# Where the small level products of a GLA head are issued: in one block, or in pieces between the steps of a tile

## The chip, the cores and the metric

The kernel runs on one core of a Trainium2 chip. The metric is the device time of one execution in microseconds (us), as the median of several runs. TensorE (PE in the profile) does matrix products, and its weight loads have an engine name of their own there (PEld). VectorE is DVE, ScalarE is ACT, GpSimd is POOL, and SyncE (SP) issues most of the weight transfers.

## The reference

One inference step of a two-layer decoder trunk, for 512 prompt tokens and 32 sample tokens (8 sequences of 4) with shared weights, in float32. Each layer is a SwiGLU block, a mixing block of three branches (mLSTM, gated linear attention, RG-LRU), an output projection, and a second SwiGLU block. The change touches gated linear attention (GLA), which has four heads with key width 128 and value width 256:

```python
def _gla(q, k, v, log_a, S0):
    ...
    def step(S, inp):
        qc, kc, vc, ac = inp
        b = jnp.cumsum(ac, axis=2)
        diff = jnp.where(causal[:, :, None], b[:, :, :, None, :] - b[:, :, None, :, :], -jnp.inf)
        A = jnp.einsum('bhtd,bhsd,bhtsd->bhts', qc, kc, jnp.exp(diff))
        o = jnp.einsum('bhts,bhsv->bhtv', A, vc) + jnp.einsum('bhtd,bhdv->bhtv', qc * jnp.exp(b), S)
        bL = b[:, :, -1]
        S_new = jnp.exp(bL)[..., None] * S + jnp.einsum('bhsd,bhsv->bhdv', kc * jnp.exp(bL[:, :, None] - b), vc)
        return S_new, o
```

The scores A have a decay for each key dimension, so they aren't one plain product of q and k.

## The kernel before, in words

All 544 tokens are kept with features on the partitions. A large weight product is made of three passes over split operands (high and low parts, `xh`, `xl`, `wh`, `wl`). Its unit is a tile: 128 output features for all 544 tokens, in 8 steps over the inner dimension, each step six matmuls of 272 columns (three passes, two halves), all at L415. `pair` holds two PSUM buffers for tiles, `stream_a` and `stream_b` in the profile, and `Q` (`mix` in the profile) is the PSUM of the attention work, four banks.

Every engine has its own order of instructions, written out by hand, and the engines meet through semaphores that count up. A weight block of 1 MB holds two tiles. SyncE loads it into `stage` when VectorE has split the block before last in that slot; ScalarE copies the high part (`split_hi`, L836), VectorE makes the low part (`split_lo`, L1154), and TensorE multiplies.

A GLA head takes four weight blocks: n (query and key tiles), n + 1 (values), n + 2 and n + 3 (four gate tiles, t + 4 to t + 7). The attention work lies between these tiles. The scores are made by levels. A chunk of 128 tokens is halved again and again, and at each level a product of decayed queries and decayed keys (`seven`, one row for each level) gives the scores across the cut. The two coarsest levels are the outer products (L690). The diagonal (`kT` and `qT`) and the five finest levels are six inner products (L698); each is 16 small matmuls of 32 by 32 outputs, 4 chunks by 4 groups of `G` = 32 rows, and each matmul shows as two records. Behind them come the sample sequences' products (L702 to L706) and a transpose of the decayed keys into rows (L710). All of this is one function, `scores`, that is called between tile t + 4 and tile t + 5. Then TensorE issues tile t + 5, waits for `b_took`, and multiplies the key rows with the values (L716) for the states; then tile t + 6 follows, and in `outputs` the next head's decays (L663), the chunk outputs (L723, L725) and the reads of the sample states (L543), which wait for `b_zin`.

VectorE waits for the pieces by `b_ring`, through `ring(0)` to `ring(3)`: it copies the outer products into `wS` (L1571), collects the inner levels with predicated copies into `inner` (L1573, L1578), copies them to `wS` (L1581), copies the key rows to `Kw` (L1583), and handles the samples (L1586 to L1590). The last of these raises `b_took`. Then it merges the previous head (L1396, L1397), takes the gate tile (L1145), updates the states (L1362, L1364), splits a block (L1154), prepares the sample keys, and takes the next head's decays (`take_decays`, L1494), which raises `b_zin`; that step reads the bank that L543 writes next.

`pair_block` already has an argument `inside`: for each of the two tiles a list of a step number and a function to call ahead of that step. The mLSTM heads and tile t + 7 of the GLA heads use it.

Of the kernel before, what the change touches and what calls it, by code (L numbers as in the profile page):

```python
# [27 lines left out]
P = 128  # L28
D = 1024
KT = D // P  # L30
# [10 lines left out]
C = 128  # L41
NC = T // C
# [3 lines left out]
NL = len(LEVELS)  # L46
SM = DV + P
NLS = 2
G = 32
NIN = sum(h < G for h in LEVELS)  # L50
# [33 lines left out]
def spread(ap, dim, n):  # L84

    shape = list(ap.shape)
    shape[dim] = n
    return ap.broadcast_to(shape)


class Chain:
# [22 lines left out]
    def link(self, ins):  # L114
        self.n += 1
        ins.then_inc(self.sem, 1)
        self.eng.wait_ge(self.sem, self.n)
# [5 lines left out]
def trunk(nc, x_T, w_up1, w_down1, w_mix, w_gates, w_o, w_up2, w_down2, vec, b_if, w_lr2, w_ra, w_ri, consts, level_masks,  # L123
          m0, c0, n0, s0, h0, conv0, o_y, o_pc, o_pm, o_ps, o_ph, o_pconv,
          o_sc, o_sn, o_sm, o_ss, o_sh, o_sconv, rows_dram):
    with ExitStack() as ctx:
# [11 lines left out]
        wh = sb("wh", [P, 2, W_SLOT], F32R)  # L138
        wl = sb("wl", [P, 2, W_SLOT], F32R)
        V = sb("vectors", [P, V_ALL])  # L140
        ones = sb("ones", [P, P])
        ident = sb("ident", [P, P])
# [46 lines left out]
        qT = sb("qT", [P, N], where=heads)  # L189
        kT = sb("kT", [P, N], where=heads)  # L190
# [3 lines left out]
        seven = sb("seven", [P, NL, N], where=heads)  # L194
        wS = sb("wS", [P, N], where=heads)
        Kw = sb("Kw", [P, NC, P], where=heads)
# [39 lines left out]
        Q = psum("mix", [P, 4, 512])  # L236
# [49 lines left out]
        b_fac, b_ring, b_took = sem("b_factors"), sem("b_ring_full"), sem("b_ring_took")  # L286
# [123 lines left out]
        def _(pe):  # L410
# [101 lines left out]
            def pair_block(n, t, j, after_first=None, inside=((), ())):  # L512

                block_ready(n)
                for e in range(2):
                    done = 0
                    for k, between in inside[e]:
                        tile(t + e, e, KT, 2 * P, e * P, weights=(wh[:, j], wl[:, j]), ks=range(done, k))
                        between()
                        done = k  # L520
                    tile(t + e, e, KT, 2 * P, e * P, weights=(wh[:, j], wl[:, j]), ks=range(done, KT))
                    if after_first and e == 0:
                        after_first()
# [143 lines left out]
            def gla_head(L, i, first=False, last=False):  # L667
                B = L * HEADS + i
                n = L * LAYER_BLOCKS + i * HEAD_BLOCKS + (BLK_MIX + HEADS * HEAD_BLOCKS)
                t = L * LAYER_TILES + i * HEAD_TILES + (TILE_MIX + GATE_TILES + HEADS * HEAD_TILES)  # L670

                if first:
                    pe.wait_ge(root_done, L * (2 * HEADS) + HEADS + 1 + i)
                    decays(B, 0)
                pair_block(n, t, 0)
                block_ready(n + 1)
                value_tiles(t + 2, 1)
                sm = slice(T, N)

                def scores():  # L680


                    pe.wait_ge(b_fac, B + 1)
                    pe.wait_ge(root_done, L * (2 * HEADS) + HEADS + 1 + i)
                    for c in range(NC):
                        for l, groups in ((0, (0, 1)), (1, (0, 2))):
                            for g in groups:
                                k0, q0 = c * C + g * G, c * C + (g // (2 - l) * (2 - l) + 2 - l if l else 2) * G
                                q1 = q0 + LEVELS[l]
                                mm = pe.matmul(Q[g * G:(g + 1) * G, 0, q0:q1], seven[:, l, k0:k0 + G],  # L690
                                               seven[:, l, q0:q1], start=True, stop=True)
                    mm.then_inc(b_ring, 1)
                    for r in range(NIN + 1):
                        lhs, rhs = (kT, qT) if r == 0 else (seven[:, NL - NIN + r - 1, :],) * 2
                        for c in range(NC):
                            for g in range(P // G):
                                k0, o = c * C + g * G, r % 4 * P + c * G
                                mm = pe.matmul(Q[g * G:(g + 1) * G, 1 + r // 4, o:o + G], lhs[:, k0:k0 + G],  # L698
                                               rhs[:, k0:k0 + G], start=True, stop=True)
                        if r == 3:  # L700
                            mm.then_inc(b_ring, 1)
                    pe.transpose(Q[0:NS, 2, 2 * P:3 * P], kh[:, sm], ident[:])  # L702
                    pe.matmul(Q[0:NS, 2, 3 * P:3 * P + NS], kT[:, sm], qT[:, sm], start=True, stop=True)
                    for e in range(NLS):
                        lv = seven[:, NL - NLS + e, sm]
                        mm = pe.matmul(Q[0:NS, 2, 3 * P + (e + 1) * NS:3 * P + (e + 2) * NS], lv, lv, start=True, stop=True)  # L706
                    mm.then_inc(b_ring, 1)
                    for c in range(NC):
                        sl = slice(c * C, (c + 1) * C)
                        mm = pe.transpose(Q[:, 3, sl], kh[:, sl], ident[:])  # L710
                    mm.then_inc(b_ring, 1)

                pair_block(n + 2, t + 4, 0, scores)
                pe.wait_ge(b_took, B + 1)
                for c in range(NC):
                    pe.matmul(Q[:, c, 0:DV], Kw[:, c, :], val[:, c, 0:DV], start=True, stop=True).then_inc(b_u, 1)  # L716

                def chunk_outputs(v):

                    vs = slice(v * P, (v + 1) * P)  # L720
                    for c in range(NC):
                        sl = slice(c * C, (c + 1) * C)
                        mm = pe.matmul(Q[:, v, sl], val[:, c, vs], wS[:, sl], start=True, stop=c == 0)  # L723
                        if c:
                            mm = pe.matmul(Q[:, v, sl], Cst[:, c - 1, vs], qs[:, sl], start=False, stop=True)  # L725
                    return mm

                def outputs():
                    pe.wait_ge(b_c, B * NC + NC)
                    if not last:  # L730
                        decays(B + 1, 2)
                    chunk_outputs(0)
                    pe.wait_ge(b_cs, B * 16 + 16)
                    if not last:
                        pe.wait_ge(b_zin, B + 2)
                    state_reads(3, b_rd)
                    chunk_outputs(1).then_inc(b_out, 1)
                    pe.wait_ge(b_rows_read, B + 1)
                    for v in range(2):
                        pe.matmul(Q[:, 2, v * NS:(v + 1) * NS], val[:, NC, v * P:(v + 1) * P], wSs[:],  # L740
                                  start=True, stop=False, skip_group_check=True)
                        mm = sample_states(2, v, v * NS)
                    mm.then_inc(b_outs, 1)
                    pe.wait_ge(b_keys, B + 1)
                    sample_updates(0, 3, b_us)

                taken = L * (8 * HEADS) + i * 4 + (4 * HEADS + 1)

                def second():
                    pe.wait_ge(b_h, B + 1)  # L750
                    sample_updates(1, 2, b_us)

                def third():
                    pe.wait_ge(b_sqs, B + 1)
                    column_sum(hsq[:, 0], 0, b_var)
                    pe.wait_ge(head_samples, taken + 1)
                    sample_updates(2, 3, b_us)

                pair_block(n + 3, t + 6, 1, outputs, ((), ((4, second), (6, third))))
                pe.wait_ge(head_samples, taken + 2)  # L760
                sample_updates(3, 2, b_us)
# [370 lines left out]
        def _(dve):  # L1132
# [370 lines left out]
            def gla_head(L, i, first=False, last=False):  # L1503
# [49 lines left out]
                def ring(r):  # L1553
                    dve.wait_ge(b_ring, B * 4 + (r + 1))

                def chunks(ap):

                    return ap.rearrange("p (c t) -> p c t", c=NC)

                def compact(r):  # L1560

                    return chunks(Q[:, 1 + r // 4, r % 4 * P:(r % 4 + 1) * P])
# [6 lines left out]
                for rows, cols_ in ((slice(0, 2 * G), slice(2 * G, P)), (slice(0, G), slice(G, 2 * G)),  # L1569
                                    (slice(2 * G, 3 * G), slice(3 * G, P))):  # L1570
                    dve.tensor_copy(av[rows, :, cols_], src[rows, :, cols_])  # L1571
                ring(1)
                link(tt_(inner[:], compact(0), spread(ident_g[:].unsqueeze(1), 1, NC), ALU.mult))  # L1573
                for r in range(1, NIN + 1):
                    if r == 4:
                        ring(2)
                        chain.hold()
                    link(dve.copy_predicated(inner[:], spread(masks[:, r - 1, :].unsqueeze(1), 1, NC), compact(r)))  # L1578
                for g in range(P // G):
                    rows = slice(g * G, (g + 1) * G)  # L1580
                    dve.tensor_copy(av[rows, :, rows], inner[rows])  # L1581
                ring(3)
                dve.tensor_copy(Kw[:], chunks(Q[:, 3, :]))  # L1583
                As = wSs[0:NS]
                s0_ = 3 * P
                link(tt_(As, Q[0:NS, 2, s0_:s0_ + NS], ident[0:NS, 0:NS], ALU.mult))  # L1586
# [320 lines left out]
```

## Time and profile before

| what | value |
|---|---|
| median of 3 runs | 3126.54 us (3124.81 to 3127.68) |
| profiled execution, its own time | 3129.91 us |
| span of that profile | 3128.1 us |
| TensorE busy | 3055.7 us (98%) |
| VectorE busy | 1902.3 us (61%) |
| ScalarE busy | 1038.8 us (33%) |
| mean granted clock of TensorE | 0.994 |
| DMA | 292.18 MB, mean 93 GB/s |

The profile is one execution. "Busy" is the time in which an engine has at least one instruction under way. The start of an instruction is measured; the end of a matmul is modelled, so distances between starts say more than durations. The granted clock is a share of 2.4 GHz. In the chain, a row gives when a piece of the chain begins, how long it is, and how many records it holds; "issue" is time in which the engine waits for nothing that the profile shows. Some matmul records are missing from the trace, so the counts of such pieces can be a little low.

### The profile page before, as it was taken

Reading aid. Unit: us, or ns where it says so; the run is one execution under the profiler, and the core shown is the slowest. Engines: PE = TensorE matmul, PEld = TensorE weight load, DVE = VectorE, ACT = ScalarE, POOL = GpSimd, SP = SyncE. Lnnn points to the kernel's source line nnn. Section 1 sums busy time; section 2 is a strip of 40 time slices with the busy share of each in tenths; the row PEclk is TensorE's granted clock in tenths of the full one; section 3 lists DMA queues with packets and bytes.
Section 4 is the critical chain, followed back from the end, with each engine's and each line's share of the span. In section 5 each row is a group of like instructions: output and inputs, shape, how many; then the busy total and the mean of one; then the engine's idle time right before and its main releaser. Section 6 shows DMA issues by size and latency. Waiting matters only on the chain.

```text
span 3128.1 us, 60370 instructions
## 1 busy us (share of the span) xinstructions
PE 3055.7 (98%) x25824; PEld 3013.2 (96%) x25824; DVE 1902.3 (61%) x2705; ACT 1038.8 (33%) x992; POOL 12.9 (0%) x36
## 2 busy tenths in 40 slices
PE   7999999999999999999999999999999999999998
PEld 7999999999999999999999999999999999999997
DVE  5434467778887874434454344776888788643344
ACT  3222232334344642212232122333334355421212
POOL 1000000000000000000000000000000000000000
PEclk9999999999999999999999999999999999999999
DMA  4222233233222222222222222233222322222222
GB/s 145 74 99 89 72 112 109 106 110 110 96 100 88 74 83 94 78 97 75 87 94 81 101 89 84 94 125 129 94 89 95 96 91 74 96 81 83 92 79 71
DMA packets 51916, 292.18 MB, mean 93 GB/s; under 512 B 9385, under 2 KB 12265, under 8 KB 23881
## 3 DMA queue, kind: packets, MB, share of 16 engines
q1 hardware_dynamic: 37152, 241.43, 22.3%
q10 hardware_dynamic: 13984, 48.48, 4.2%
q8 instruction: 90, 1.47, 0.2%
q0 software_dynamic: 656, 0.52, 0.1%
q14 instruction: 34, 0.27, 0.0%
HBM read 268.90 MB, written 21.50 MB: 93 GB/s over the span
## 4 chain that ended last, share of the span: by engine, by line
PE 84%; DVE 9%; ACT 4%; issue 2%; DMA 1%; ACTq 0%; DVEq 0%; POOL 0%; POOLq 0%
PE stream_b L415 36%; PE stream_a L415 35%; PE stream_a L502 4%; DVE wl L1154 1%; DVE xc L1653 1%; ACT wh L836 1%; PE stream_b L508 1%; PE mix L622 1%; PE mix L562 1%; PE mix L723 1%; PE mix L543 1%; PE mix L625 1%; ACT L1059 0%; PE mix L555 0%; PE mix L698 0%
## 5 line engine op out<-in xcount | busy, mean ns | idle before, releaser
L836 ACT ACTIVATE wh<-stage 128x2048 fp32r<-128x2048 f32 (+2 forms) x246 | 435.8, 1772 | 773.9 <-PE stream_b L415 561.3
L1154 DVE TENSOR_TENSOR wl<-stage,wh 128x2048 fp32r<-128x2048 f32 (+2 forms) x248 | 525.8, 2120 | 112.2 <-ACT wh L836 88.4
L415 PE MATMUL stream_a<-xh,wh 128*128 128x272 f32 x2560 | 537.5, 291 | 27.0 <-DVE xl L1160 13.0
L415 PE MATMUL stream_b<-xh,wh 128*128 128x272 f32 x2560 | 538.3, 291 | 2.1 <-issue 1.2
L415 PE MATMUL stream_a<-xl,wh 128*128 128x272 f32 x2560 | 531.3, 289 | 0.0
L415 PE MATMUL stream_b<-xl,wh 128*128 128x272 f32 x2560 | 531.3, 289 | 0.0
L415 PE MATMUL stream_a<-xh,wl 128*128 128x272 f32 x2560 | 529.8, 288 | 0.0
L415 PE MATMUL stream_b<-xh,wl 128*128 128x272 f32 x2560 | 529.7, 288 | 0.0
L415 PEld LDWEIGHTS stream_a<-xh,wh 128*128 128x128 f32 x2560 | 404.6, 189 | 31.3 <-DVE wl L1154 13.0
L415 PEld LDWEIGHTS stream_b<-xh,wh 128*128 128x128 f32 x2560 | 405.4, 189 | 8.4 <-issue 3.7
L415 PEld LDWEIGHTS stream_b<-xh,wl 128*128 128x128 f32 x2560 | 404.1, 189 | 1.0 <-issue 1.0
L415 PEld LDWEIGHTS stream_a<-xh,wl 128*128 128x128 f32 x2560 | 404.1, 189 | 0.0
L415 PEld LDWEIGHTS stream_a<-xl,wh 128*128 128x128 f32 x2560 | 401.5, 190 | 0.0
L415 PEld LDWEIGHTS stream_b<-xl,wh 128*128 128x128 f32 x2560 | 401.5, 190 | 0.0
L1145 DVE TENSOR_TENSOR us<-stream_b,rstd 128x544 f32<-128x544 f32 x88 | 63.8, 725 | 446.6 <-PE stream_b L415 446.5
L893 ACT ACTIVATE sg<-gs 128x544 f32<-128x544 f32 x88 | 58.1, 660 | 400.6 <-DVE gs L1145 400.6
L415 PE MATMUL stream_a<-hh,wh 128*128 128x272 f32 x704 | 145.9, 289 | 0.0
L415 PE MATMUL stream_b<-hh,wh 128*128 128x272 f32 x704 | 145.9, 289 | 0.0
L415 PE MATMUL stream_a<-hh,wl 128*128 128x272 f32 x704 | 145.7, 288 | 0.0
L415 PE MATMUL stream_b<-hh,wl 128*128 128x272 f32 x704 | 145.7, 288 | 0.0
L502 PE MATMUL stream_a<-wh,xl 128*128 128x256 f32 x512 | 144.7, 283 | 0.0
L415 PE MATMUL stream_b<-hl,wh 128*128 128x272 f32 x704 | 144.1, 286 | 0.0
(349 smaller groups left out, 4360.9 us busy)
## 6 DMA issues: line engine op xcount, KB each, us to landing
stage<-in_w_mix SPq DMA_DIRECT2D x88, 1024.0 KB, 4.8
stage<-in_w_up SPq DMA_DIRECT2D x87, 1024.0 KB, 4.8
stage<-in_w_down SPq DMA_DIRECT2D x32, 768.0 KB, 4.2
stage<-in_w_down SPq DMA_DIRECT2D x32, 640.0 KB, 3.9
CS<-in_c ACTq DMA_DIRECT2D x8, 1024.0 KB, 4.7
out_o_sc<-CS ACTq DMA_DIRECT2D x8, 1024.0 KB
CS<-in_s ACTq DMA_DIRECT2D x8, 1024.0 KB, 4.8
out_o_ss<-CS ACTq DMA_DIRECT2D x8, 1024.0 KB
```

The source lines that it names most:

```text
L415: mm = [pe.matmul(out(h), a(h), b(h), start=f, stop=z) for h in range(2)]
L502: mm = pe.matmul(out, a[:, k, tok], b[:, j, k * DV:(k + 1) * DV], start=f, stop=z)
L508: mm = pe.matmul(pair[1][:, 0, 0:DV], both[:, k * 2 * NS:k * 2 * NS + P], b[:, j, k * DV:(k + 1) * DV], start=f, stop=z)
L543: mm = pe.matmul(Q[g * NS:(g + 1) * NS, b_, 0:DV], Qm[:, s_ * NS:(s_ + 1) * NS], CS[:, s_, :], start=s_ < 4, stop=s_ >= 4)
L562: mm = pe.matmul(Q[:, b_ + h, 0:HALF], ones[:], src[:, h * HALF:(h + 1) * HALF], start=True, stop=True)
L622: mm = pe.matmul(Q[:, v, sl], here, wS[:, sl], start=True, stop=c == 0)
L625: mm = pe.matmul(Q[:, v, sl], before, qs[:, sl], start=False, stop=True)
L723: mm = pe.matmul(Q[:, v, sl], val[:, c, vs], wS[:, sl], start=True, stop=c == 0)
L836: act.activation(wh[:, slot, 0:width], stage[:, slot, 0:width], ACT.Copy).then_inc(hi_done, 1)
L893: act.activation(sg[:], gs[:], ACT.Silu).then_inc(silu_done, 1)
L1145: ins = tt_(halves(dst), banks(pair[slot]), rs2, ALU.mult)
L1154: tt_(wl[:, slot, 0:width], stage[:, slot, 0:width], wh[:, slot, 0:width].bitcast(F32), ALU.subtract).then_inc(split_done, 1)
```

## The change

The six inner products, the outer products, the samples and the key rows become functions of their own. The outer products are still issued between tile t + 4 and tile t + 5 (ahead of step 0). The rest goes between the steps of tile t + 5, the fifth counted from zero: key rows and the diagonal ahead of step 1, level 1 ahead of step 2, levels 2 and 3 ahead of step 3, level 4 ahead of step 4, level 5 and the samples ahead of step 5. So the key rows, which were last, are second. On VectorE the copy of the key rows moves ahead of the inner levels, and `ring` counts on accordingly. Levels 4 and 5 still wait for the signal that comes behind the samples. The formula of `q0` is written in another form with the same values.

```diff
@@ pair_block
                     for k, between in inside[e]:
-                        tile(t + e, e, KT, 2 * P, e * P, weights=(wh[:, j], wl[:, j]), ks=range(done, k))
+                        if k > done:
+                            tile(t + e, e, KT, 2 * P, e * P, weights=(wh[:, j], wl[:, j]), ks=range(done, k))
                         between()
                         done = k
@@ gla_head of TensorE
-                def scores():
-
+                def outer():
 
                     pe.wait_ge(b_fac, B + 1)
                     pe.wait_ge(root_done, L * (2 * HEADS) + HEADS + 1 + i)
...
                     mm.then_inc(b_ring, 1)
-                    for r in range(NIN + 1):
...
+
+                def rows_of_keys():
+
+                    for c in range(NC):
+                        sl = slice(c * C, (c + 1) * C)
+                        mm = pe.transpose(Q[:, 3, sl], kh[:, sl], ident[:])
+                    mm.then_inc(b_ring, 1)
+
+                def inner_level(r):
+
+                    lhs, rhs = (kT, qT) if r == 0 else (seven[:, NL - NIN + r - 1, :],) * 2
+                    for c in range(NC):
+                        for g in range(P // G):
+                            k0, o = c * C + g * G, r % 4 * P + c * G
+                            mm = pe.matmul(Q[g * G:(g + 1) * G, 1 + r // 4, o:o + G], lhs[:, k0:k0 + G],
+                                           rhs[:, k0:k0 + G], start=True, stop=True)
+                    if r == 3:
+                        mm.then_inc(b_ring, 1)
+
+                def samples():
+
...
                     mm.then_inc(b_ring, 1)
-                    for c in range(NC):
-                        sl = slice(c * C, (c + 1) * C)
-                        mm = pe.transpose(Q[:, 3, sl], kh[:, sl], ident[:])
-                    mm.then_inc(b_ring, 1)
-
-                pair_block(n + 2, t + 4, 0, scores)
+
+                pair_block(n + 2, t + 4, 0, None,
+                           ((), ((0, outer), (1, rows_of_keys), (1, lambda: inner_level(0)), (2, lambda: inner_level(1)),
+                                 (3, lambda: inner_level(2)), (3, lambda: inner_level(3)), (4, lambda: inner_level(4)),
+                                 (5, lambda: inner_level(5)), (5, samples))))
@@ gla_head of VectorE
                 ring(1)
+                dve.tensor_copy(Kw[:], chunks(Q[:, 3, :]))
+                ring(2)
                 link(tt_(inner[:], compact(0), spread(ident_g[:].unsqueeze(1), 1, NC), ALU.mult))
                 for r in range(1, NIN + 1):
                     if r == 4:
-                        ring(2)
+                        ring(3)
                         chain.hold()
...
-                ring(3)
-                dve.tensor_copy(Kw[:], chunks(Q[:, 3, :]))
```

## Rows read from the trace of the kernel before

**Rows 1.** The page: the instruction queue's packets, and the chain by engine
```profile
q8 instruction: 90, 1.47, 0.2%
...
PE 84%; DVE 9%; ACT 4%; issue 2%; DMA 1%; ACTq 0%; DVEq 0%; POOL 0%; POOLq 0%
```

**Rows 2.** Waits of TensorE: total us, times, longest
```profile
PE mix L698 <- issue: 9.1, 4, 3.5
```

**Rows 3.** TensorE in windows, L690 to L716 of heads: length, busy, clock, DMA share
```profile
782.43:795.82 13.39, 11.35 (x285) 0.87 0.23 81
849.49:859.11 9.62, 9.62 (x285) 1.00 0.30 109
912.57:923.47 10.90, 9.96 (x285) 1.00 0.29 99
...
2455.72:2471.50 15.78, 12.32 (x284) 0.78 0.20 69
sum 94.35, PE 84.06; mean PE 10.51
```

**Rows 4.** Chain, second and third head of layer 0: start us, us, what
```profile
784.80 2.04 issue
...
788.36 7.45 PE stream_b L415 x48
...
853.08 6.02 PE stream_b L415 x48
```

**Rows 5.** All engines in a window behind the second head's gap; clock behind POOL
```profile
789.60:791.30 1.70, 1.70 (x9) 1.70 (x9) 1.55 (x6) 0.00 (x0) 0.00 (x0) 0.50 0.00 0
```

**Rows 6.** Chain, fourth head of layer 0
```profile
919.48 0.94 issue
```

**Rows 7.** DMA queues, 784.4 to 785.5: packets, MB, share of 16 engines
```profile
q8 instruction: 1, 0.02, 5.6%
```

**Rows 8.** DMA, fourth head: a window, packets of 914 to 918, queue of 918 to 919.3
```profile
916.00:917.00 1.00, 1.00 (x11) 1.00 (x9) 0.83 (x3) 0.00 (x0) 0.00 (x0) 1.00 1.00 426
...
q1 hardware_dynamic: 132, 1.05, 74.5%
...
q8 instruction: 1, 0.02, 4.5%
```

**Rows 9.** Timeline of TensorE: start us, us, what, records merged into a row
```profile
533.05 0.52 PE L415 MATMUL stream_b<-xh,wh 128*128 128x272 f32 x2
533.41 0.42 PE L415 MATMUL stream_b<-xh,wl 128*128 128x272 f32 x2
...
787.39 0.29 PE L706 MATMUL mix<-seven 128*32 128x32 f32 x4
787.61 0.75 PE L710 MATMUL mix<-ident,sq 128*128 128x128 f32 x4
...
858.95 0.81 PE L716 MATMUL mix<-val,Kw 128*128 128x256 f32 x3
...
869.65 1.07 PE L543 MATMUL mix<-CS,Qm 128*32 128x256 f32 x16
...
912.16 0.41 PE L415 MATMUL stream_a<-xl,wh 128*128 128x272 f32 x2
912.50 0.73 PE L690 MATMUL mix<-seven 128*32 128x64 f32 x24
```

**Rows 10.** Timeline of VectorE, second and third head of layer 0
```profile
787.81 0.64 DVE L1578 COPY_PREDICATED inner<-masks,mix 128x128 f32<-128x128 int32 x2 [1.06 <-PE mix L706]
...
854.27 0.64 DVE L1578 COPY_PREDICATED inner<-masks,mix 128x128 f32<-128x128 int32 x2 [0.22 <-DVE inner L1578]
...
855.87 0.69 DVE L1583 COPY Kw<-mix 128x512 f32<-128x512 f32 x1
...
857.22 0.28 DVE L1590 COPY Kf<-mix 32x128 f32<-32x128 f32 x1
...
868.77 0.78 DVE L1494 TENSOR_SCALAR seven<-mix,vectors 128x544 f32<-128x544 f32 x1 [0.25 <-DVE K L1332]
```

More of the change, by code:

```diff
@@ L687, in scores @@
                             for g in groups:
-                                k0, q0 = c * C + g * G, c * C + (g // (2 - l) * (2 - l) + 2 - l if l else 2) * G
+                                k0, q0 = c * C + g * G, c * C + (g + 1 if l else 2) * G
                                 q1 = q0 + LEVELS[l]
@@ L692, in scores @@
                     mm.then_inc(b_ring, 1)
-                    for r in range(NIN + 1):
-                        lhs, rhs = (kT, qT) if r == 0 else (seven[:, NL - NIN + r - 1, :],) * 2
-                        for c in range(NC):
[L696 to L700, printed above, removed]
-                            mm.then_inc(b_ring, 1)
+                def rows_of_keys():
[13 more added lines that the diff above has]
+                def samples():
                     pe.transpose(Q[0:NS, 2, 2 * P:3 * P], kh[:, sm], ident[:])
@@ L707, in scores @@
                     mm.then_inc(b_ring, 1)
-                    for c in range(NC):
-                        sl = slice(c * C, (c + 1) * C)
-                        mm = pe.transpose(Q[:, 3, sl], kh[:, sl], ident[:])
-                    mm.then_inc(b_ring, 1)
-                pair_block(n + 2, t + 4, 0, scores)
+                pair_block(n + 2, t + 4, 0, None,
+                           ((), ((0, outer), (1, rows_of_keys), (1, lambda: inner_level(0)), (2, lambda: inner_level(1)),
+                                 (3, lambda: inner_level(2)), (3, lambda: inner_level(3)), (4, lambda: inner_level(4)),
+                                 (5, lambda: inner_level(5)), (5, samples))))
                 pe.wait_ge(b_took, B + 1)
```

## The prediction

> **What bounds the kernel now.** I read the page first, then the waits of TensorE, then the chain, stretch by stretch. The chain of work that ended last is 84% TensorE [rows 1], so time is gained or lost only where TensorE stops, runs slowly, or gets work in a dearer order. The change touches one stretch of each GLA head, eight in all (four heads, two layers): from the first outer product (T0 below) to the update products at L716. The waits show that in it the small products at L698 stand idle 9.1 us by "issue", that is, without waiting for another engine [rows 2]. Eight windows give the stretch of each head [rows 3]: 94.35 us together. The third head of a layer is the clean one: 9.62 us, TensorE busy throughout. The worst takes 15.78. Two kinds of loss make that up. The chain of layer 0's second head shows a gap of 2.04 us inside L698, and then the tile takes 7.45 us, where the third head's takes 6.02 [rows 4]; in that tile the granted clock is 0.50, the 1.2 GHz level [rows 5]. The fourth head's gap of 0.94 us [rows 6] left the clock at 1.00 [rows 3].
>
> What are the gaps? In the second head one packet of the instruction queue lands inside 784.4 to 785.5, and the products go on at 786.84, 1.3 us or more later [rows 4, 7]. In the fourth head the weight load fills the DMA engines (share 1.00 from 916 to 917); the 132 packets of 914 to 918 are all its own, one of instructions comes in 918 to 919.3, and TensorE, which had stopped at 919.48, goes on 0.94 us later, at 920.42 [rows 6, 8]. I read this as TensorE running out of code: 192 inner records at L698 go by in under 2 us where nothing holds them, against 6.02 us for a tile's 48 [rows 4], and a fetch asked for during the weight load is served behind it. The Trainium skill, page "Runtime: NRT & Kernel Launch", section "Instruction fetch mechanics", has blocks of 16 KiB with 256 instructions, fetched while the last is executed, and calls the cost mostly hidden; this trace has a packet of that size (1.47 MB in 90) [rows 1], but the cost isn't hidden here.
>
> **Term A, removed.** With the clean head as the floor, eight times 9.62 is 76.96, so 94.35 - 76.96 = 17.4 us are gaps, slow clock and restarts. Spreading the products between steps of a tile (six matmul records, 0.75 us each) gives the fetch time. If all of it goes, the change earns 17.4 us; if the gaps only move, 0.
>
> **Term B, added: changes between narrow and full products.** The small products use 32 columns of the array, the tile 128. Stream matmuls start 0.125 us apart. Into narrow ones, the pair that starts at 912.16 makes the next due at 912.41, and L690 starts at 912.50: 0.09 late [rows 9]. Back out, the four records at L706 start 0.03 apart from 787.39 on, the last at 787.48, and L710 follows at 787.61: 0.13, of which about 0.01 to 0.03 is the narrow record's own slot, so 0.11. The second full matmul is late too: behind the narrow state reads of the other branch the pair at 533.05 is followed at 533.41, 0.36 where 0.25 is usual, another 0.11 [rows 9]. A round trip costs 0.09 + 0.11 + 0.11 = 0.31 us. Before there is one a head. Afterwards there are six: outer; level 0; level 1; levels 2 and 3; level 4; level 5 with the samples. The key rows have full width and add none. Five more cost 1.55 us a head, 12.4 us in all. The bounds are 0.2 and 0.4 a round trip (8 and 16 us), since after short narrow records only the first delay is seen, and there before a transpose. The Trainium skill, "TensorEngine Tiling (Array Packing)", section "Tiling Modes", says that changing the tiling mode drains the engine; the trace agrees, with the 0.09 and 0.11 above, and this is the rule that speaks against the change.
>
> **Term C, added: the wait for b_took.** Today VectorE finishes the level products at 857.50 (L1590), 1.45 us before L716 starts at 858.95 [rows 9, 10]. The change puts the samples and level 5 after step 5, with three steps behind them. VectorE now waits with levels 4 and 5 until ring(3). From L1578's last pair (854.27) to L1590's end (857.50) is 3.23 us; the key copy at L1583, 0.69 and its gap, moves ahead, leaving 2.53. It starts 0.20 us after the first full matmul behind the samples (787.61 to 787.81) [rows 9, 10] and its signal takes 0.04: 2.77 us. TensorE's 18 records take 2.26 + 0.11 = 2.37. It waits 0.40 us a head, 3.2 in all. The earlier key copy buys nothing here beyond what is counted. Bounds: 0 and 0.7 a head.
>
> **Term D, added: the wait for the next head's decays.** Behind b_took VectorE merges the previous head (two large operations), takes the gate tile, updates the states, splits a weight block, prepares the sample keys and only then takes the decays at L1494. L1590's end to L1494's end is 12.05 us (857.50 to 869.55) [rows 10]. TensorE goes from L716 (858.95) to the state reads at L543 (869.65) in 10.70 us [rows 9], and those wait for that very signal (b_zin). Today VectorE's lead of 1.45 us covers it with 0.10 us left. With the lead gone (L716 starts 0.04 after L1590's end) L543 is due 10.74 after it and allowed 12.09 after it: 1.35 us. The first head of a layer merges with one operation, not two, and just makes it; the last has no decays to take. So four waits, 5.4 us. Behind L543 VectorE has idle time again, since it waits for TensorE's outputs before it can evict, so the delay isn't handed on. Bounds: 0 and 8.
>
> **Term E, what stays of A.** The weight load still starts when VectorE has split its block; in the fourth head all its 1.05 MB lie in 914 to 918 [rows 8], from T0 + 1.4 to T0 + 5.4. A block of code ends at a fixed count of instructions, and those of four or five steps and of the keys now come ahead of it. In three heads (second of layer 0, first and fourth of layer 1) the gap came late among the products or behind them; in the new order the same count is reached in level 4 or later, at about T0 + 6.8: outer products 0.7, four steps 3.0, key rows 0.45, four levels at 0.31 (six in under 2 us), four round trips 1.2, and a bit of level 4. Its code is asked for while the load runs, and then it is usable at T0 + 7.9, as in the fourth head (912.57 to 920.42 [rows 3, 6]). That leaves 1.1 us in each of three heads, 3.3 us. Bounds: 0, and the 10 us of gaps that there are today (9.1 and 0.94 [rows 2, 6]).
>
> **Sum.** - 17.4 + 12.4 + 3.2 + 5.4 + 3.3 = + 6.9 us. The sum is made on the profiled execution, 3129.91 us (span 3128.1, 1.8 around it), which is 0.1% over the median, 3126.54; a difference carries over: 3126.5 + 6.9 = 3133.4 us.
>
> **Rivals.**
> 1. The code comes in time everywhere: term E is 0, +3.6, 3130.1 us. For it: blocks take longer to use up, and TensorE queues ahead during steps. Against: the load is still in the middle of the stretch. 22%.
> 2. VectorE's waits C and D don't come, because it does its work in less than I add up: 12.4 + 3.3 - 17.4 = - 1.7, 3124.8 us. Against: 0.10 us of lead at L543. 8%.
> 3. Faster, the other side: round trips are hidden behind the 0.125 us of a stream matmul. It decides at 0.06 us a round trip (2.5 us in all): at 0, with E at 0, the sum is - 17.4 + 8.6 = - 8.8, 3117.7 us. For it: nothing but the many gaps in term A, and that 0.31 was read with other neighbours. 12%.
> 4. The remaining gaps and the drained array together let the clock drop again. One drop costs 7.45 - 6.02 = 1.4 us; in three heads 4.3, 3137.7, in all eight 11.4, 3144.8 us. For it: gap and waits of 1 to 1.4 us now lie within one stretch. 14%.
> 5. The gaps aren't cured, the pieces only move them: A gives nothing, E is out, + 21.0, 3147.5 us. 5%.
>
> **How the numbers follow.** The forecast itself holds 39%, between 3130 and 3137. Some 0.2%, 6.3 us, is what a measurement of this kernel can tell from no change. Faster by more: rival 3 and a little of rival 2, 13%. Within it: rival 1, most of rival 2 and under half of the forecast, 40%. Slower: the rest of the forecast, rivals 4 and 5 and a little of rival 1, 47%. The range leaves out rival 5, the far end of rival 4 and about half of rival 3: 3121 to 3143.
>
> **What would show it.** Right: L698's issue waits fall from 9.1 to 2 to 4 us; no clock drop in the eight stretches; each L415 pair behind a narrow piece is followed 0.36 us later; a clean stretch grows from 9.62 to about 11.6 us; L716 waits for VectorE's L1590 copy about 0.4 us in every head, and L543 for L1494 about 1.35 us in the second and third head of each layer. Wrong: a clean stretch near 10 us would refute term B, no wait at L543 term D, issue gaps of 2 us and slow clock term A. If the level products were taken in an order that let VectorE finish as early as now, terms C and D would go and the change would be nearly free.

## The result, and the profile after

The changed kernel takes 3140.18 us (median of 6 runs, 3139.67 to 3141.29); the kernel before, in the same comparison, 3124.56 us (6 runs, 3122.94 to 3127.68). The ratio is 1.0051, with a 95% interval of 1.0040 to 1.0061: 15.6 us slower, beyond the 0.2% that can be told from no change. The profiled execution of the changed kernel took 3140.60 us (span 3138.8).

In it the lines of the file have moved: the inner products are L707 (L698 before), the key rows L698 (L710), the key-and-value products L727 (L716), the state reads L544 (L543), VectorE's last sample copy L1601 (L1590) and the decays L1505 (L1494).

The waits of TensorE answer to [rows 2]; the columns are total us, times, longest:

```profile
PE mix L544 <- DVE seven L1505: 4.7, 4, 1.2
PE mix L707 <- issue: 3.4, 3, 1.5
...
PE mix L727 <- DVE Kf L1601: 2.1, 7, 0.3
```

The issue gaps inside the products fell from 9.1 to 3.4 us, and two waits for VectorE are new. The eight stretches, from the first outer product to the key-and-value products, answer to [rows 3]; the columns are length, TensorE busy, granted clock, DMA share, GB/s:

```profile
...
783.25:797.39 14.14, 12.66 (x284) 0.88 0.22 76
852.57:864.07 11.50, 11.25 (x284) 1.00 0.26 91
...
2269.05:2281.82 12.77, 11.41 (x283) 1.00 0.24 85
...
2468.66:2481.34 12.68, 11.43 (x284) 1.00 0.26 86
sum 97.18, PE 91.69; mean PE 11.46
```

A clean stretch now takes 11.50 us instead of 9.62. Three are more than 1 us longer: they still have a gap, of 1.48, 1.04 and 0.92 us. Only the second head of layer 0 still loses clock. The chain in it shows how the pieces lie, and the gap that stayed:

```profile
784.07 0.94 PE stream_b L415 x6
785.01 0.44 PE mix L698 x4
785.45 0.39 PE mix L707 x32
...
790.09 1.48 issue
791.57 0.28 PE mix L707 x9
```

A step of six records, 0.75 us in an unbroken tile, takes 0.94 to 0.96 us between narrow pieces. The timeline gives the distances between starts, to be held against [rows 9]:

```profile
855.10 0.52 PE L415 MATMUL stream_b<-xh,wh 128*128 128x272 f32 x2
855.46 0.41 PE L415 MATMUL stream_b<-xh,wl 128*128 128x272 f32 x2
855.71 0.41 PE L415 MATMUL stream_b<-xl,wh 128*128 128x272 f32 x2
856.05 0.46 PE L707 MATMUL mix<-seven 128*32 128x32 f32 x32
```

The pair behind the narrow piece is followed 0.36 us later, not 0.25, and the piece starts 0.34 us behind the last pair, where 0.25 would be due: the distances that the prediction took from other places hold here.

### The profile page after: what moved, and what is told of

Its sections match the earlier page's. It is cut to its first block, busy times and chain, and to the rows that moved or that the text cites. A ratio compares the mean times of both kernels' runs of the same rounds, so it can differ in the third digit from the quotient of the medians.

```text
span 3138.8 us, 60370 instructions
## 1 busy us (share of the span) xinstructions
PE 3067.1 (98%) x25824; PEld 3015.6 (96%) x25824; DVE 1902.4 (61%) x2705; ACT 1039.3 (33%) x992; POOL 12.9 (0%) x36
## 3 DMA queue, kind: packets, MB, share of 16 engines
q8 instruction: 90, 1.47, 0.2%
## 4 chain that ended last, share of the span: by engine, by line
PE 82%; DVE 11%; ACT 4%; issue 2%; DMA 1%; DVEq 0%; ACTq 0%; POOL 0%; POOLq 0%
PE stream_b L415 35%; PE stream_a L415 34%; PE stream_a L502 4%; DVE wl L1165 1%; ACT wh L847 1%; DVE xc L1664 1%; PE stream_b L508 1%; PE mix L623 1%; PE mix L563 1%; PE mix L707 1%; PE mix L544 1%; PE mix L626 1%; ACT L1070 0%; PE mix L556 0%; PE mix L734 0%
## 5 line engine op out<-in xcount | busy, mean ns | idle before, releaser
L415 PE MATMUL stream_a<-hl,wh 128*128 128x272 f32 x704 | 144.1, 286 | 0.0
```

The costliest lines, as they stand in the source:

```text
L415: mm = [pe.matmul(out(h), a(h), b(h), start=f, stop=z) for h in range(2)]
```

## The experiments

**The kernel before, profiled again.** No edit.

> The kernel before, unchanged, profiled once more. The profile of the kernel before took 3129.91 us, 5.3 us over the median of its six runs (3124.56), while that of the changed kernel lay 0.4 us over its own. Theory: the profile of before held more fetch gaps than usual, so term A (17.4 us) was read too large. Then this profile comes out near 3124 to 3126 us, and its eight stretches from L690 to L716 add up to 88 to 91 us instead of 94.35, the difference lying in issue gaps and slow clock. Rival: the 5 us lie elsewhere in the program, and the eight stretches add up to 94 us again.

It took 3126.91 us. The last of its windows, that of layer 1's fourth head, and the sum:

```profile
2453.39:2468.51 15.12, 11.36 (x285) 0.89 0.20 72
sum 91.04, PE 80.77; mean PE 10.10
```

The edges of some of these windows lie up to 0.2 us inside the stretch. Read off the chain, where the windows of [rows 3] begin and end, the sum is 91.49 us, 2.9 less than in [rows 3], with a time that is 3.0 us less. Two more profiles that were meant for other questions (code_shifted and before_decays_early, below) have stretches that are the same work: read off the chain they add up to 90.06 and 87.20 us, at 3125.56 and 3123.52 us. So in four profiles the time falls by 6.4 us where the stretches fall by 7.2. As far as four profiles can tell, most of the spread of this kernel, 3121.25 to 3129.79 us over the comparisons here, is fetch gaps and what the clock loses behind them. The profile that the prediction read was from the slow end. At the median of 3124.56 us the stretches should be about 89 us and term A 89 - 77 = 12 us, not 17.4.

**Key rows second, nothing spread.**

```diff
-                pair_block(n + 2, t + 4, 0, None, ((), (...)))
+                def scores():
+                    outer()
+                    rows_of_keys()
+                    for r in range(NIN + 1):
+                        inner_level(r)
+                    samples()
+
+                pair_block(n + 2, t + 4, 0, scores)
```

> The changed kernel with its functions called in one block between the two tiles again, in the new order: outer products, key rows, six inner products, samples. Against the kernel before only the order differs: the full-width key rows stand between two narrow pieces, one more round trip a head. Theory (a round trip costs 0.31 us): a clean stretch grows from 9.62 to 9.9 us, eight times 0.3 make +2.4 us, the fetch gaps stay, no new wait at L716 or L544. Time +2 to +3 us. Rival (round trips are cheap, and the 15.6 us of the change are the waits for VectorE): +0.

It took 3132.78 us, ratio 1.0023 (1.0013 to 1.0033), + 7.2 us. The third head's chain, which is clean:

```profile
851.51 0.81 PE mix L690 x26
...
861.44 0.65 PE mix L732 x3
```

851.51 to 861.44 is 9.93 us, 0.31 over the 9.62 of before: one round trip at the forecast price. Eight make 2.5 of the 7.2 us. For the rest there is one profile, of an execution 2.6 us over the median. In it the eight stretches add up to 96.66 us, 17.2 over eight clean ones, where the kernel before has about 12: layer 1's fourth head alone has a gap of 4.67 us, and its tile then takes 8.59. So the gaps were worse there, but how much of the median's 7.2 us they are is not shown. The order of full and narrow pieces was priced right; that it also touches the gaps was not in my expectation.

**The decays early.**

```diff
-                masked_keys(Kf[0:NS], None if last else lambda: take_decays(L, i + 1, 2)).then_inc(b_keys, 1)
+                if not last:
+                    take_decays(L, i + 1, 2)
+                masked_keys(Kf[0:NS]).then_inc(b_keys, 1)
```

> The changed kernel, but VectorE takes the next head's decays (L1505 there) ahead of preparing the sample keys instead of in its middle. Theory (term D): the four waits of 1.2 us at L544 go and nothing takes their place, so 4 to 5 us are given back: about 3135.5 us, +11 us to the kernel before. Rival (TensorE would wait for the sample keys instead, which come 0.8 us later): the wait moves from L544 to L556 and less than 1 us is given back.

3134.47 us (6 runs, 3134.23 to 3134.95): 5.7 us less than the changed kernel's 3140.18, ratio to before 1.0031 (1.0019 to 1.0044). No wait for the decays at L544 is left in its profile, and none for the sample keys came. The two kernels were timed in two comparisons; each against its own kernel before (15.6 and 8.9 us slower), the gain is 6.7 us. Term D is shown: VectorE's late decays cost 5 to 6 us, and one moved step gives them back.

**The same edit on the kernel before.**

> The kernel before with the next head's decays taken ahead of the sample keys, nothing else. Control for two_pieces and three_pieces, which have this edit too. Theory: the kernel before has no wait for the decays, so it gains nothing, 0 to 1 us. Rival (part of what these kernels gain over the kernel before is this edit): 3 us or more faster.

3124.38 us, ratio 1.0001 (0.9991 to 1.0010): nothing, as the lead of VectorE there covers the decays. So the edit alone explains none of what follows.

**Three narrow pieces,** with the decays early.

```diff
-                           ((), ((0, outer), (1, rows_of_keys), (1, lambda: inner_level(0)), (2, lambda: inner_level(1)),
-                                 (3, lambda: inner_level(2)), (3, lambda: inner_level(3)), (4, lambda: inner_level(4)),
-                                 (5, lambda: inner_level(5)), (5, samples))))
+                           ((), ((0, outer), (0, lambda: inner_level(0)), (0, lambda: inner_level(1)), (2, rows_of_keys),
+                                 (2, lambda: inner_level(2)), (2, lambda: inner_level(3)), (4, lambda: inner_level(4)),
+                                 (4, lambda: inner_level(5)), (4, samples))))
```

> The changed kernel with decays early and the products in three narrow pieces instead of six: outer, levels 0 and 1 ahead of step 0; key rows, levels 2 and 3 ahead of step 2; levels 4, 5 and samples ahead of step 4. Theory: three round trips fewer (8 x 3 x 0.31 = 7.4 us), the wait at the key-and-value products (L727 in the changed kernel) gone because four steps now cover VectorE's 2.8 us (3 us), the wait at L544 gone (4.7 us): about 3125 us, level with the kernel before, unless fetch gaps come back (up to 4 us). Rival (spreading itself is dear, through the clock or the fetch): it stays within 3 us of decays_early, near 3133.

3120.66 us (11 runs), ratio 0.9988 (0.9979 to 0.9997): 4.9 us under the kernel before, where I had expected level with it. The chain of the third head:

```profile
845.47 0.78 PE mix L690 x24
846.25 0.61 PE mix L707 x47
846.86 1.71 PE stream_b L415 x12
848.57 0.44 PE mix L698 x4
...
855.82 1.30 PE mix L727 x6
```

10.35 us, 0.73 over 9.62 for two more round trips. Its waits show 0.4 us of issue in all. That is less than the changed kernel's 3.4, though the products are denser. What made it better than expected is that not only did no gap come back, those of the changed kernel went too: its stretches hold 5.2 us more than eight clean ones (97.18 against 8 x 11.50), those of this profile 0.85 (83.65 against 8 x 10.35). In the third head the first two levels are over at 846.86, and the DMA engines move nothing from 845.4 to 848. Whether that timing is why the gaps went was not tested.

**Three pieces, the decays late.**

> Three pieces, but VectorE takes the next head's decays where the changed kernel does, in the middle of the sample keys. Theory (term D holds in this order too): from the end of the copy at L1601, 9.9 us behind the first outer product, 12.05 us pass to the decays, and the state reads at L544 are due at 20.97: a wait of 1.0 us in the second and third head of each layer, 4 us in all, about 3124.7 us. Rival (four steps behind the samples give VectorE enough lead): no wait, 3120.7 us.

3124.45 us (11 runs), ratio 0.9997 (0.9988 to 1.0006): 3.8 us over three_pieces by the medians, 2.8 by the ratios, as the two were timed in different comparisons. It has this row of waits:

```profile
PE mix L544 <- DVE seven L1505: 3.8, 4, 1.0
```

Four waits of 1.0 us, as worked out. The wait at the key-and-value products (term C) is gone here, the wait for the decays is not, so the two have thresholds of their own.

**Two narrow pieces,** with the decays early.

```diff
+                           ((), ((0, outer), (0, lambda: inner_level(0)), (0, lambda: inner_level(1)),
+                                 (0, lambda: inner_level(2)), (3, rows_of_keys), (3, lambda: inner_level(3)),
+                                 (3, lambda: inner_level(4)), (3, lambda: inner_level(5)), (3, samples))))
```

> As three_pieces, but in two narrow pieces: outer and levels 0 to 2 ahead of step 0; key rows, levels 3 to 5 and samples ahead of step 3. Theory: one round trip fewer than three_pieces gives 8 x 0.31 = 2.5 us, a clean stretch is 9.9 us; but 256 instructions can now go by in under 2 us in the first piece, so one gap of up to 1.5 us can come back in a head or two. 3118 to 3122 us. Rival (two round trips are already enough against the gaps and the rest is noise): 3118.

3116.75 us (6 runs, 3116.39 to 3118.94), ratio 0.9970 (0.9958 to 0.9982): the best of all, 8.4 us under the kernel before of its comparison (3125.18) and 23 us under the changed one. Its third head:

```profile
845.99 0.78 PE mix L690 x25
846.77 0.88 PE mix L707 x63
847.65 2.45 PE stream_b L415 x18
850.10 0.44 PE mix L698 x4
...
856.00 1.73 PE mix L727 x8
```

10.01 us, 0.39 over before. One gap of 0.6 us is left in the products of the whole kernel, in a profile whose execution (3118.94 us) was the slowest of the six. The median came out below the 3118 that even the rival gave. Apart from that gap, three steps in the middle are enough for the fetches here.

**The code moved, first try.** 128 register moves ahead of each layer's mixing block.

> The kernel before with 128 register moves added to TensorE's program ahead of each layer's mixing block. Nothing in a GLA head changes but where its instructions lie in the program: by 128 in layer 0, by 256 in layer 1. Theory (the gaps are fetches of code in blocks of 256 instructions): in the second head of layer 0 the gap, which had 0.32 us of L698 left behind it, comes 128 instructions earlier, with about 0.9 us left; the fourth head's gap, which lay in the middle of the tile, moves into the products and grows; in layer 1, shifted by a whole block, the second head's gap stays where it was, with about 0.7 us of L698 left, and so does the fourth's, with 0.4. Rival (the gaps come from the products or from the weight load, not from the program's addresses): every gap stays where it was in both layers.

The moves are not in the compiled program: the page has 90 packets of the instruction queue and 1.47 MB, as before [rows 1], while the second try below, with as many instructions more, has 92 and 1.51 MB. So this says nothing on the theory and is a further run of the kernel before, with the lines numbered otherwise: 3125.56 us, and the gaps where they were.

**The code moved, second try.**

```diff
-                for c in range(NC):
+                for c in list(range(NC)) * 9:
                     pe.matmul(Q[:, 2, c:c + 1], acc[:, c * C:(c + 1) * C], ones[:, 0:1], start=True, stop=True)
```

> The kernel before with 32 extra products at L533 ahead of each layer's mixing block (each of its four small products is issued nine times, with the same values), which are 128 instructions that stay in the program. The register moves of code_shifted had been dropped when it was compiled, so that program was the one before. Theory (the gaps are fetches of code in blocks of 256 instructions): everything behind lies 128 instructions later in layer 0 and 256 in layer 1. In layer 0 the gap comes 128 instructions, 0.6 us of L698, earlier in a head: the second head's with 0.9 us of L698 left behind it instead of 0.32, the fourth head's inside L698 instead of in the middle of the tile. In layer 1, shifted by a whole block, the second head's gap stays with 0.73 us left and the fourth's with 0.3 to 0.4. Rival (the gaps hang on the products or on the weight load, not on the program's addresses): every gap stays where it was in both layers.

It took 3149.62 us, and the 25 us more are the added products (last section); the question is only where the gaps lie. In the chain of the unmoved program (code_shifted, whose L702 is L698 elsewhere), first the second head of layer 0, and that of layer 1:

```profile
784.70 1.96 issue
786.66 0.32 PE mix L702 x13
...
2326.36 1.83 issue
2328.20 0.73 PE mix L702 x48
```

The same in the moved one, and its fourth head of layer 0:

```profile
797.99 0.73 issue
798.72 0.89 PE mix L698 x58
...
925.75 1.85 issue
927.61 0.45 PE mix L698 x25
...
2351.61 1.90 issue
2353.50 0.73 PE mix L698 x48
```

In layer 0, moved by 128 instructions, 0.89 us of products are left behind the gap instead of 0.32 (forecast: 0.9), and the fourth head's gap lies inside the products. In layer 1, moved by 256, 0.73 us are left as before. The first head of layer 0 did what the expectation did not say. In code_shifted its gap has 0.75 us of L702 (L698 elsewhere) behind it; moved, it comes later, behind all of L698 and behind L702:

```profile
733.91 1.85 issue
735.76 0.22 PE mix L703 x2
```

With a period of 256, 128 instructions earlier and 128 later are the same place, and only the later one lies in this head's products. The gaps follow the program's addresses with a period that 256 instructions fit: they are fetches of code.

The DMA queues say the same. In each of 37 such gaps, from nine of the traces, one packet of the instruction queue starts 2.2 to 3.9 us before TensorE goes on; how long it takes is its share of the window times 16 engines. From the packet's end to TensorE's next product 1.3 to 1.7 us pass in 36 of them, 0.9 in one.

The Trainium skill, "Runtime: NRT & Kernel Launch", section "Instruction fetch mechanics", gives blocks of 256 instructions; the run agrees with the length, while its word that the fetch is mostly hidden doesn't hold for dense narrow products.

**The weight load later.**

```diff
                 dve.memset(t8[:], 0.0).then_inc(b_fac, 1)
-                split_lo(n + 3, 1, 2 * D)
                 take_gate(L, i, t + 4, 0, 0, acts, "silu", None)
...
                 dve.wait_ge(b_took, B + 1)
+                split_lo(n + 3, 1, 2 * D)
```

> The kernel before, with VectorE's split of the weight block n + 3 moved from ahead of the level products to behind them, which moves the start of the 1 MB load that it frees from 2.5 us behind the first outer product to about 8 us, out of the products. Theory (a fetch asked for during the load waits behind it): the gaps of 2.0 us in the second heads stay, since a block of 256 instructions still goes by in less than a fetch takes; the gap in layer 0's fourth head (0.94 us in one profile) goes, and that of layer 1's fourth head shrinks from 3.5 to 2.0 us, with its slow clock. 3 us faster, and the spread between runs smaller. Rival (the load has nothing to do with it): the gaps stay as they are, no change.

3127.61 us (11 runs), ratio 1.0009 (1.0000 to 1.0018): not faster. Layer 0's fourth head has no gap, but with the load where it was before_again and code_shifted have none there either. Layer 1's fourth has 2.10 us instead of 3.46, but before_decays_early has 1.99 there. The issue waits inside the products are 8.1 us in both. Part of the time went into a new wait of 2.3 us for the decays, since VectorE's split of 2.3 us now stands ahead of them. The time of this run settles nothing on the load; that the second heads' gaps stay at 2 us without it is clear.

The traces say more. The gap of layer 1's fourth head begins at the same place of the program, with 0.3 to 0.4 us of products behind it, in the kernel before, before_again, code_shifted, before_decays_early and here. Here no packet of the load is near, and the packet of instructions starts 0.4 us before the gap (2457.0 to 2457.2). In the kernel before it starts as early, but the load begins 0.2 us behind it (2457.6 to 2457.8). The share is that of 16 engines in a window of 0.2 us, so the packet takes 0.9 us here and 2.3 us there:

```profile
q8 instruction: 1, 0.02, 27.4%
```

```profile
q8 instruction: 1, 0.02, 72.3%
```

code_shifted is like the kernel before: a packet of 2.1 us and a gap of 3.20 us. In before_again the load has begun first; the packet takes 0.9 us but starts 1.2 us after the gap has begun, and the gap is 3.76 us. In keys_second, whose order differs, it starts behind the whole load, 2.3 us after the gap has begun: 4.67 us. So the load does lengthen a fetch that meets it, by stretching its packet or by putting it off, by 1.1 to 2.6 us at this place; in before_decays_early, where the packet took 1.6 us, it added nothing.

## Why the prediction was right, and what was off

The direction and the mechanism held; the size was 6.9 us where 15.6 were measured.

*Term A, removed (17.4 us)* is the term that was off, in its size and in the sentence of the sum that "a difference carries over" to the median. The time above the clean floor was read from one execution, 5.3 us over its own median, in a kernel whose runs spread by 8 us, most of it, as far as four profiles tell, through this term. Worth about 12 us at the median, it moves the forecast to + 12 us. Between the two profiled executions the difference is 3140.60 - 3129.91 = 10.7 us, against 6.9 forecast. The 3133.4 us also stood on a median of three runs, 3126.54, where six give 3124.56.

The other terms are best read from the starts of records, as the prediction did. A stretch of [rows 3] ends where the modelled end of the last tile record lies, and the waits of the profile count from there too. In the clean third head of layer 0 the first outer product starts at 849.42 and the tile behind the key-and-value products at 860.49; in the changed kernel 852.50 and 865.72. First the kernel before:

```profile
860.49 0.60 PE L415 MATMUL stream_a<-xh,wh 128*128 128x272 f32 x2
```

```profile
865.72 0.60 PE L415 MATMUL stream_a<-xh,wh 128*128 128x272 f32 x2
```

That is 11.07 and 13.22 us, 2.15 more, where the windows show 1.88. Of it 1.63 are round trips, 0.41 the wait for b_took, and 0.11 a slower run of the key-and-value products behind a wait (1.65 us from their start to the tile's, instead of 1.54), which no term had.

*Term B, round trips (12.4 us).* Right, a little small: 1.63 us for five in the changed kernel is 0.33 each, 13.0 in all. 0.31 us in keys_second, 0.73 for two with three_pieces and 0.39 for one with two_pieces.

*Term C, the wait for b_took (3.2 us).* Right in place, cause and size. In the third head VectorE starts on levels 4 and 5 only behind the samples' signal, having waited 1.99 us for it (timeline of VectorE; start, length, what it does, and its wait in brackets):

```profile
861.49 0.64 DVE L1591 COPY_PREDICATED inner<-masks,mix 128x128 f32<-128x128 int32 x2 [1.99 <-PE mix L718]
...
863.74 0.28 DVE L1601 COPY Kf<-mix 32x128 f32<-32x128 f32 x1
```

and TensorE starts when that ends (timeline of TensorE):

```profile
863.41 0.41 PE L415 MATMUL stream_b<-xl,wh 128*128 128x272 f32 x2
...
864.07 0.48 PE L727 MATMUL mix<-val,Kw 128*128 128x256 f32 x1 [0.25 <-DVE Kf L1601]
```

Behind the pair that starts at 863.41 the next record is due at 863.66; it comes 0.41 us late, and the forecast was 0.40. Over the eight heads this makes 3.2 us: 0.41 to 0.50 in seven, and almost nothing in the second head of layer 0, where the slow clock held TensorE back. The 2.1 us in the row of waits are less only because they count from the modelled end of the last matmul.

*Term D, the wait for the decays (5.4 us).* Right. From the key-and-value products to the state reads 12.06 us pass, 10.70 before; 0.11 of the difference is the slower run above, so the wait is 1.25 us, 5.0 us over the four waits in the second and third head of each layer (4.7 in the row of waits). From the end of VectorE's last sample copy to the end of the decays 12.05 us pass, as forecast. VectorE's decays end at 876.07 in the third head, and TensorE goes on at once; first VectorE's timeline, then TensorE's:

```profile
875.29 0.78 DVE L1505 TENSOR_SCALAR seven<-mix,vectors 128x544 f32<-128x544 f32 x1 [0.25 <-DVE K L1343]
```

```profile
876.13 0.64 PE L544 MATMUL mix<-CS,Qm 128*32 128x256 f32 x8 [1.18 <-DVE seven L1505]
```

*Term E, the rest of the gaps (3.3 us).* The three heads were the right ones, with gaps of 1.48, 1.04 and 0.92 us where 1.1 was forecast, and the first of them comes 6.8 us behind the first outer product, in level 4, as forecast. The sum is 97.18 - 8 x 11.50 = 5.2 us. The excess is the second head of layer 0, 2.6 us, where the gap of 1.48 us was followed by slow clock. This window lies behind the gap (length, busy, clock, DMA share, GB/s):

```profile
791.60:793.20 1.60, 1.60 (x15) 0.64 0.04 10
```

In the 1.5 us behind that window the clock is 0.50. So rival 4 came in one head of eight, and the sign "no clock drop in the eight stretches" failed there. That head's fetch came as forecast, behind the load. From 785.8 to 789.2 the packets are the load's alone, and the fetch is among those of 789.3 to 790.4 (DMA queues of the two stretches; packets, MB, share):

```profile
q1 hardware_dynamic: 138, 1.01, 78.8%
```

```profile
q8 instruction: 1, 0.02, 5.5%
```

That the load delays a fetch is read from such traces and from those of layer 1's fourth head above; the time of the run that moved the load doesn't show it.

With A at 12, clean heads at 17.2 (8 x 2.15, which holds B, C and the slower run behind the wait), D at 5.0 and E at 5.2 the sum is + 15.4 us, against 15.6 measured. That it meets so closely is partly luck: A at the median is good to about 1 us, and the interval of the measured ratio reaches from 12.5 to 19.1 us.

Of the rivals, 1 (all code in time) fell with the three gaps that are left, 3 (hidden round trips) with keys_second, 2 with the waits at L727 and L544, 5 with the issue gaps, 3.4 us instead of 9.1. The closing remark of the prediction, that without C and D the change would be nearly free, was too kind: decays_early still loses 8.9 us.

## What to carry to other kernels

Spreading dense small products between the steps of a large one cures gaps of code fetch, but each round trip between full and narrow products costs TensorE 0.31 to 0.39 us here, so use as few pieces as end the gaps: two, with the decays moved early as well, gained 0.3% where the changed kernel's six lost 0.5%. Place the last piece by the engine that reads it: count its work from the last product to the signal that TensorE waits for next, and to the one after that. Where a term of the sum is idle time that varies from run to run, read it from more than one profile, or scale it to the median, before it is set against fixed costs. Measure what a stretch costs from start to start, beyond the wait at its end: windows that end at the wait missed 0.27 us a head here.

## What was not expected of the hardware

The clock fell although TensorE was busy throughout, from 7 us before the added products on. The 32 added products of one column in code_shifted_2 make the 8 records at L533, 0.78 us in the kernel before, 72 records that take 13.21 us in the chain:

```profile
425.89 13.21 PE mix L533 x72
```

and the granted clock in them falls to the 1.2 GHz level (length, busy, clock, DMA share, GB/s):

```profile
...
431.00:435.00 4.00, 4.00 (x20) 0.50 0.00 0
```

Up to 427 it is 1.00, and at 428, 2 us into these products, 0.50. At 0.18 us a record they are nearly twice as dear as the eight. That is why this run is of use for the place of its gaps alone. The other surprise is how much the fetch of code varies: the same program's gap in layer 1's fourth head was 3.46, 3.76 and 3.20 us and, with one step of VectorE moved, 1.99 us.
